# A hybrid decoder step on one core: the cached values multiplied unsplit in full precision, instead of as high and low parts

## The chip, the cores and the metric

The kernel runs on one core of a Trainium2 chip. TensorE (PE) multiplies, VectorE (DVE), ScalarE (ACT) and GpSimd (POOL) work element by element, SyncE (SP) issues most transfers. Each engine takes its own instructions in order, and the engines wait for one another through semaphores. The metric is the device time of one execution in microseconds (us); lower is better. The kernel before took 1194.81 us, the median of three runs (1193.85 to 1203.77).

## The reference

One layer of a decoder serves 512 prompt tokens and 8 sample sequences of one new token each. After a norm and one input projection, two mixers run side by side, and their results are gated, merged, projected and sent through an MLP. The part that matters here is the second mixer of the samples: softmax attention over 2048 cached positions (16 pages of 128), of which each head of each sequence sees the three best blocks of 256.

```
scores = einsum('bhqd,bhnd->bhqn', qh, k_mean);  top_k(scores, 3)
p = softmax(concat([q . k_selected, q . k_own]) * HD_B ** -0.5)
o = einsum('bhqkl,bhqkld->bhqd', p_sel, v_sel) + einsum('bhql,bhld->bhqd', p_own, v_own)
```

All is float32. There are 8 heads of 64, so a page of values is 128 positions x 512. The first mixer, a gated delta rule over the 512 prompt tokens in 4 chunks of 128 and 4 heads of 128, runs on the engines in the same stage.

## The kernel before, in words

The program has these stretches. The input units (29 of them, each a 1024 x 128 slice of weights times 520 columns) come first, to about 225 us. Prompt attention follows, with the products of cached keys and queries on POOL and their sums on DVE, to 344 us. Then come gates, the choice of blocks and the exponentials of the sample scores, to 394 us. Then the stage that the change touches, from 403 to 623 us: the four chunks of the delta rule, with the 64 value groups woven in. After it come the remaining gates with the sample recurrence, the merge, the output projection and the MLP.

Large products use a split: every weight tile `w_raw` is copied by ACT to `w_high` (type float32r, `split_high`, L400) and DVE writes the rest, `w_low` (`split_low`, L405). A product is then three float32r matmuls per slice (`product`, L416): high times high, high times low, low times high. Tiles of type float32, without such a split, are multiplied directly; the trace shows each of these matmuls as two records, while a float32r matmul is one.

The cached values go the same way. `ring` has four slots; each holds a group of two pages (2 x 128 x 512). SP loads a group (L509, L494) once its slot is free. For each group:

- ACT copies it to `v_high` (L827), which has two buffers,
- POOL (even groups, L574) or DVE (odd groups, L1261) writes `v_low`, the difference, and this frees the slot,
- PE multiplies both parts (L1782). The stationary operand is `wz`, 128 columns wide: the first 16 are the high and low parts of the 8 heads' unnormalised probabilities of that page, the rest are whatever follows them. The moving operand is 512 columns of `v_high` or `v_low`. That makes four matmuls a group.

After the 8 groups of a sequence, DVE keeps of the 16 x 512 sums the 64 columns of each row's own head (L1275), and PE adds the rows up by 4 small matmuls (`turn_values`, L1763).

The order is written out by hand. `delta_order` lists the stages of the delta rule for chunks 0 and 2 in one slot and 1 and 3 in the other, the second slot four steps behind. After the stages that `VALUES` names, each engine takes one value group; what is left of the 64 comes at the end of the stage. In the delta rule each `left` (4 matmuls, 128 columns each) needs DVE's last update of `Em` (L1333), and each `right` (8 matmuls) needs ACT's copy of `left` to `sqb` (L867); all of these are L1795 on PE.

The buffers `v_high` and `v_low` lie in the memory of `w_raw`. For this reason the weights of gates 8 to 11 are loaded from ACT's queue only after the last value matmul (`load_last_gates`), and gate 8 follows when they are split. `wz`, `sqb` and one of the buffers for the sums lie in the memory of `w_high` and `w_low`.

Of the kernel before, what the change touches and what calls it, by code (L numbers as in the profile page):

```python
# [26 lines left out]
ALU = mybir.AluOpType  # L27
# [135 lines left out]
def hybrid_step(nc, const_f, const_m, x_prompt, x_sample, cache_k, cache_v, page_table, state_delta, state_conv,  # L163
# [9 lines left out]
    with ExitStack() as ctx:  # L173
# [11 lines left out]
        v_high = at("v_high", [P, 2, 2 * WB], F32R, pos[0] - 16384)  # L185
        v_low = at("v_low", [P, 2, 2 * WB], F32R, pos[0] - 8192)
# [5 lines left out]
        wz = at("wz", [P, 2048 + 128], F32R, split_at + 4096)  # L192
# [125 lines left out]
        def bc(ap, shape):  # L318
# [21 lines left out]
            hw_out yf_sums yf_root yf_inv ys_out ys_done y_act y_dve v_scaled vb_masked vb_turned vb_out diag_out v_high_out v_low_pool v_low_dve""".split()  # L340
# [5 lines left out]
                lg_biased row_sums den_out gc_out ssr_in wz_low row_head sm_conv sm_ms sm_bd sm_decay sm_dlt sm_bdo  # L346
                sm_oms sm_on os_ready os_l inv_ready""".split(),
            "scalar": """sig_out sp_out tail_out lg_exp own_exp egc_out ssr_out wz_high wz_end sm_silu sm_root sm_bdin
# [15 lines left out]
        def done(name):  # L364

            engine, i = once_at[name]
            return once_sem[engine], i + 1
# [75 lines left out]
        def low_done(i):  # L443


            return S["v_low_dve" if i % 2 else "v_low_pool"], i // 2 + 1
# [7 lines left out]
        def _(sp):  # L454
# [47 lines left out]
            for r in range(8):  # L502
                if r < 4:
                    sp.wait_ge(S["k_red"], GROUPS - 3 + r)
                else:
                    sp.wait_ge(*low_done(r - 4))
# [45 lines left out]
        def _(g):  # L552
# [14 lines left out]
            values_done = [0]  # L567

            def values(n):

                for i in range(values_done[0], min(values_done[0] + n, GROUPS)):
                    if i % 2 == 0:
                        g.wait_ge(S["v_high_out"], i + 1)
                        g.tensor_tensor(v_low[:, i % 2], ring[:, i % 4].rearrange("p g c -> p (g c)"),  # L574
                                        v_high[:, i % 2].bitcast(F32), ALU.subtract).then_inc(S["v_low_pool"], 1)
                values_done[0] += n
# [18 lines left out]
            values(GROUPS)  # L595
# [9 lines left out]
        def _(act):  # L605
# [196 lines left out]
            for c in range(NCH):  # L802
# [9 lines left out]
            A(wz[:, 0:2048].rearrange("p (b g a h) -> p b g a h", b=NS, g=NPAGE, a=2)[:, :, :, 0],  # L812
              lg[:].rearrange("p b h g -> p b g h"), ACT.Copy).then_inc(*did("wz_high"))
            A(wz[:, 2048:], cf[:, K_ONE:K_ONE + P], ACT.Copy).then_inc(*did("wz_end"))

# [3 lines left out]
            values_done = [0]  # L819

            def values(n):

                for i in range(values_done[0], min(values_done[0] + n, GROUPS)):
                    act.wait_ge(kv_landed[i % 4], 32 * (2 * NS + i // 4 + 1))
                    if i >= 2:
                        act.wait_ge(S["pv_done"], i - 1)
                    A(v_high[:, i % 2], ring[:, i % 4].rearrange("p g c -> p (g c)"), ACT.Copy)\  # L827
                        .then_inc(S["v_high_out"], 1)
                values_done[0] += n
# [7 lines left out]
            values(1)  # L837
            taken, loaded = 0, False
            for stage, c in delta_order():
# [3 lines left out]
                values(VALUES.get(stage.rstrip("0123456789"), 0))  # L843
                if taken >= GROUPS and not loaded:
                    load_last_gates()
                    loaded = True
                taken += VALUES.get(stage.rstrip("0123456789"), 0)
# [39 lines left out]
            values(GROUPS)  # L887
            if not loaded:
                load_last_gates()


# [90 lines left out]
        def _(v):  # L982
# [259 lines left out]
            def head4(ap):  # L1242
                return ap.rearrange("p (h d) -> p h d", h=HA)

            v.wait_ge(*done("wz_high"))
            parts = wz[:, 0:2048].rearrange("p (b g a h) -> p b g a h", b=NS, g=NPAGE, a=2)
            TT(parts[:, :, :, 1], lg[:].rearrange("p b h g -> p b g h"), parts[:, :, :, 0].bitcast(F32), ALU.subtract)\
                .then_inc(*did("wz_low"))

            row_head = s5[0:2 * HB, 0:HB]  # L1250
            TT(row_head, cf[0:2 * HB, K_ID:K_ID + HB], cf[0:2 * HB, K_ID + HB:K_ID + 2 * HB], ALU.add)\
                .then_inc(*did("row_head"))
            v.wait_ge(*done("row_head"))
            values_done, lows_done = [0], [0]

            def lows(n):

                for i in range(lows_done[0], min(lows_done[0] + n, GROUPS)):
                    if i % 2:
                        v.wait_ge(S["v_high_out"], i + 1)  # L1260
                        TT(v_low[:, i % 2], ring[:, i % 4].rearrange("p g c -> p (g c)"),  # L1261
                           v_high[:, i % 2].bitcast(F32), ALU.subtract).then_inc(S["v_low_dve"], 1)
                lows_done[0] += n

            def values(n):

                for i in range(values_done[0], min(values_done[0] + n, GROUPS)):
                    b, r = divmod(i, 8)
                    lows(1)
                    if r == 7:  # L1270

                        v.wait_ge(S["pv_done"], i + 1)
                        if b >= 2:
                            v.wait_ge(S["vb_turned"], b - 1)
                        TT((vb0, vb1)[b % 2][0:2 * HB].rearrange("r (h d) -> r h d", d=DB),  # L1275
                           bank(2 + b % 2, WB, 2 * HB).rearrange("r (h d) -> r h d", d=DB),
                           bc(row_head.rearrange("r (h o) -> r h o", o=1), [2 * HB, HB, DB]), ALU.mult)\
# [9 lines left out]
            lows(1)  # L1287
# [245 lines left out]
        def _(pe):  # L1533
# [225 lines left out]
            def turn_values(b):  # L1759

                pe.wait_ge(S["vb_masked"], b + 1)
                for c in range(4):
                    last = mm(bank(2 + b % 2)[:, c:c + 1], (vb0, vb1)[b % 2][0:2 * HB, c * P:(c + 1) * P],  # L1763
                              cf[0:2 * HB, K_ONE:K_ONE + 1], start=True, stop=True, skip_group_check=True)
                last.then_inc(S["vb_turned"], 1)

            def values(n):
# [3 lines left out]
                for g in range(values_done[0], min(values_done[0] + n, GROUPS)):  # L1771
# [3 lines left out]
                    pe.wait_ge(*low_done(g))  # L1775
                    if g == 0:
                        pe.wait_ge(*done("wz_end"))
                        pe.wait_ge(*done("wz_low"))
                    for i in range(2):
                        first = (b * NPAGE + 2 * r + i) * 2 * HB  # L1780
                        for v_part in (v_high, v_low):
                            last = mm(bank(2 + b % 2), wz[:, first:first + P],  # L1782
                                      v_part[:, g % 2, i * WB:(i + 1) * WB],
                                      start=(r == 0 and i == 0 and v_part is v_high),
                                      stop=(r == 7 and i == 1 and v_part is v_low), skip_group_check=True)
# [230 lines left out]
```

## Time and profile before

| | |
|---|---|
| median of three runs | 1194.81 us |
| the profiled execution, its own time | 1196.35 us |
| span of its instructions | 1194.5 us |
| mean granted TensorE clock in it | 0.938 |
| PE busy | 1087.3 us (91%) |
| DVE, ACT, POOL busy | 648.0, 468.7, 256.4 us |
| the value matmuls L1782, 256 of them | 61.3 and 54.2 us busy |
| `v_high` copies L827, 64 | 67.2 us |
| `v_low` on POOL L574, 32 | 80.3 us |

Busy time of PE overlaps between neighbouring matmuls, because their ends are modelled; the distance from one start to the next tells what one costs in a stream. The granted clock is given as a share of 2.4 GHz, so 0.50 is 1.2 GHz. The profiled execution took 1.5 us more than the median.

### The profile page before, as it was taken

To read this page: it belongs to the slowest core of one execution; us is meant where nothing else is said; L and a number is where in the kernel's file an instruction comes from. 1 tells how busy PE (TensorE), PEld (TensorE's weight loads), DVE (VectorE), ACT (ScalarE), POOL (GpSimd) and SP (SyncE) were. 2 spreads that over 40 slices of the span, in tenths; PEclk is the share of its full clock that TensorE was granted. 3 is DMA by queue.
4 is the path that set the end of the run, shared out by engine and by line. 5 is a ranking of instruction groups with operands and counts; after the bars stand their busy time and mean duration, and the time that the engine had idled before them with its cause. 6 is when DMAs were issued, how large, how long until landed. Compare 5 with 4: busy or idle time off the path is not lost.

```text
span 1194.5 us, 21266 instructions
## 1 busy us (share of the span) xinstructions
PE 1087.3 (91%) x8054; PEld 1013.5 (85%) x8054; DVE 648.0 (54%) x892; ACT 468.7 (39%) x707; POOL 256.4 (21%) x113
## 2 busy tenths in 40 slices
PE   6999899698988589879968999999999999999997
PEld 6999799665677479668758799999999999999997
DVE  5228987897725774676544426555433433433443
ACT  6423554324333544554534122234413413523443
POOL 0035566776300353353330000000000000000000
PEclk8999899858998899989978899999999999999999
DMA  8376777655410245644547115433333332223311
GB/s 283 93 238 197 247 222 208 202 163 169 139 38 1 53 141 150 178 132 141 161 135 190 53 44 170 127 105 89 89 89 89 99 96 88 88 88 90 100 56 72
DMA packets 179256, 152.67 MB, mean 128 GB/s; under 512 B 8913, under 2 KB 141723, under 8 KB 178918
## 3 DMA queue, kind: packets, MB, share of 16 engines
q1 hardware_dynamic: 137414, 124.72, 35.5%
q10 hardware_dynamic: 41768, 26.91, 7.9%
q8 instruction: 52, 0.85, 0.3%
q14 instruction: 22, 0.18, 0.0%
HBM read 142.77 MB, written 8.93 MB: 127 GB/s over the span
## 4 chain that ended last, share of the span: by engine, by line
PE 76%; DVE 11%; ACT 5%; issue 4%; POOL 2%; ACTq 1%; DVEq 0%; POOLq 0%
PE ps L416 57%; PE ps L1795 6%; PE ps L1782 3%; DVE lg L1029 2%; POOL v_low L574 2%; PE ps L1682 1%; PE ps L1696 1%; DVE w_low L405 1%; PE ps L1539 1%; PE ps L1672 1%; ACTq L390 1%; DVE v_low L1261 1%; ACT v_high L827 1%; PE ps L1902 1%; ACT w_high L400 1%
## 5 line engine op out<-in xcount | busy, mean ns | idle before, releaser
L400 ACT ACTIVATE w_high<-w_raw 128x1024 fp32r<-128x1024 f32 x125 | 132.5, 1060 | 423.1 <-PE ps L416 399.8
L416 PE MATMUL ps<-xh,w_high 128*128 128x256 f32 x1216 | 257.5, 294 | 13.3 <-DVE w_low L405 7.4
L405 DVE TENSOR_TENSOR w_low<-w_raw,w_high 128x1024 fp32r<-128x1024 f32 x125 | 160.4, 1284 | 193.9 <-ACT w_high L400 193.6
L416 PE MATMUL ps<-xl,w_high 128*128 128x256 f32 x1216 | 250.0, 288 | 0.0
L416 PE MATMUL ps<-xh,w_low 128*128 128x256 f32 x1216 | 249.6, 287 | 0.0
L416 PEld LDWEIGHTS ps<-xh,w_high 128*128 128x128 f32 x1216 | 193.3, 194 | 21.1 <-issue 20.2
L416 PEld LDWEIGHTS ps<-xl,w_high 128*128 128x128 f32 x1216 | 193.7, 193 | 0.0
L416 PEld LDWEIGHTS ps<-xh,w_low 128*128 128x128 f32 x1216 | 193.6, 193 | 0.0
L557 POOL TENSOR_TENSOR ring<-ring,qb 128x1024 f32<-128x1024 f32 x64 | 158.5, 2488 | 158.7 <-DMA ring<-in_cache_k 87.0
L416 PE MATMUL ps<-mh,w_high 128*128 128x256 f32 (+1 forms) x640 | 129.3, 283 | 2.4 <-issue 2.4
L416 PE MATMUL ps<-mh,w_low 128*128 128x256 f32 (+1 forms) x640 | 129.5, 284 | 0.0
L416 PE MATMUL ps<-ml,w_high 128*128 128x256 f32 (+1 forms) x640 | 129.5, 284 | 0.0
L574 POOL TENSOR_TENSOR v_low<-ring,v_high 128x1024 fp32r<-128x1024 f32 x32 | 80.3, 2510 | 202.6 <-ACT v_high L827 202.6
L599 POOL TENSOR_TENSOR ys<-ys,rstd 8x1024 f32<-8x1024 f32 x1 | 1.9, 1886 | 566.8 <-DVE rstd L1523 566.8
L416 PEld LDWEIGHTS ps<-mh,w_high 128*128 128x128 f32 x640 | 99.8, 189 | 2.5 <-issue 2.5
L416 PEld LDWEIGHTS ps<-ml,w_high 128*128 128x128 f32 x640 | 99.9, 189 | 0.0
L416 PEld LDWEIGHTS ps<-mh,w_low 128*128 128x128 f32 x640 | 99.7, 189 | 0.0
L827 ACT ACTIVATE v_high<-ring 128x1024 fp32r<-128x1024 f32 x64 | 67.2, 1053 | 43.3 <-PE ps L1782 43.0
L1782 PE MATMUL ps<-v_high,wz 128*128 128x512 f32 x128 | 61.3, 479 | 18.1 <-DVE v_low L1261 9.0
L1029 DVE TENSOR_REDUCE lg<-ring 128x16 f32<-128x1024 f32 x64 | 76.2, 1211 | 0.1
L1502 DVE TENSOR_TENSOR ht<-ps,ht 128x520 f32<-128x520 f32 x32 | 22.4, 700 | 98.2 <-PE ps L416 98.2
L1782 PE MATMUL ps<-v_low,wz 128*128 128x512 f32 x128 | 54.2, 424 | 0.0
(358 smaller groups left out, 1498.0 us busy)
## 6 DMA issues: line engine op xcount, KB each, us to landing
ring<-in_cache_k SPq DMA_DIRECT2D x128, 256.0 KB, 3.0
ring<-in_cache_v SPq DMA_DIRECT2D x128, 256.0 KB, 2.9
w_raw<-in_w_in ACTq DMA_DIRECT2D x74, 256.0 KB, 4.0
w_raw<-in_w_up SPq DMA_DIRECT2D x64, 256.0 KB, 3.1
w_raw<-in_w_down SPq DMA_DIRECT2D x64, 256.0 KB, 2.9
w_raw<-in_w_in SPq DMA_DIRECT2D x16, 256.0 KB, 7.4
w_raw<-in_w_out SPq DMA_DIRECT2D x16, 256.0 KB, 3.0
ht_dram<-ht ACTq DMA_DIRECT2D x1, 2080.0 KB, 14.2
```

Source lines behind the costliest of these rows:

```text
L390: eng.dma_start(w_raw[:, u % 4, 4 * half:4 * half + 4, :], src).then_inc(w_landed[u % 4], 16)
L400: act.activation(w_high[:, u % 2], w_raw[:, s], ACT.Copy).then_inc(S_hi, 1)
L405: dve.tensor_tensor(w_low[:, u % 2], w_raw[:, u % 4], w_high[:, u % 2].bitcast(F32), ALU.subtract).then_inc(S_lo, 1)
L416: last = pe.matmul(out[:, a:b], w[:, u % 2, k, :], x[:, i, a:b], start=(first + i == 0 and w is w_high and x is rhs_h), stop=(first + i == ...
L557: g.tensor_tensor(ring[:, r % 4], ring[:, r % 4], bc(qb[:, b:b + 1, :], [P, 2, WB]), ALU.mult)\
L574: g.tensor_tensor(v_low[:, i % 2], ring[:, i % 4].rearrange("p g c -> p (g c)"), v_high[:, i % 2].bitcast(F32), ALU.subtract).then_inc(S[" ...
L827: A(v_high[:, i % 2], ring[:, i % 4].rearrange("p g c -> p (g c)"), ACT.Copy)\
L1029: v.tensor_reduce(lg[:, b, :, 2 * r:2 * r + 2].rearrange("p h g -> p g h"), ring[:, i % 4].rearrange("p g (h d) -> p g h d", d=DB), AX.X, ...
L1261: TT(v_low[:, i % 2], ring[:, i % 4].rearrange("p g c -> p (g c)"), v_high[:, i % 2].bitcast(F32), ALU.subtract).then_inc(S["v_low_dve"], 1)
L1502: TT(ht[:, j], unit_ps((U_MLP + i) % 2), ht[:, j], ALU.add).then_inc(S["h_out"], 1)
L1782: last = mm(bank(2 + b % 2), wz[:, first:first + P], v_part[:, g % 2, i * WB:(i + 1) * WB], start=(r == 0 and i == 0 and v_part is v_high) ...
L1795: last = mm(bank(out)[:, h * P:(h + 1) * P], left(h), right(h), start=(i == 0), stop=(i == len(pairs) - 1), skip_group_check=True)
```

## The change

The values are multiplied as they come. `v_high`, `v_low` and `wz` go, with ACT's 64 copies, the 32 subtractions on POOL and the 32 on DVE, the two copies and one subtraction that fill `wz`, and the small sum that makes `row_head`. PE waits for the landed transfer itself. The stationary operand is the 8 probabilities `lg[:, b, :, page]`, 8 columns with a step of 16 elements, the moving operand the 512 float32 columns of a page: two float32 matmuls a group instead of four float32r matmuls. Their sums have 8 rows, not 16. A slot of the ring is free when PE has multiplied it (`pv_done`). Since `w_raw` is free during the stage, ACT issues the weight loads of gates 8 to 11 before it.

```diff
-        v_high = at("v_high", [P, 2, 2 * WB], F32R, pos[0] - 16384)
-        v_low = at("v_low", [P, 2, 2 * WB], F32R, pos[0] - 8192)
-        wz = at("wz", [P, 2048 + 128], F32R, split_at + 4096)
-        def low_done(i):
-            return S["v_low_dve" if i % 2 else "v_low_pool"], i // 2 + 1
+        def slot_free(i):
+            return S["pv_done"], i + 1
...
                     if b is not None:
-                        taken, count = low_done(r + 4)
-                        sp.wait_ge(taken, b * 4 + (count - 4))
+                        sp.wait_ge(S["pv_done"], b * 8 + (r - 3))
...
-            values(1)
             for stage, c in delta_order():
-                values(VALUES.get(stage.rstrip("0123456789"), 0))
...
-            A(wz[:, 0:2048]...[:, :, :, 0], lg[:].rearrange("p b h g -> p b g h"), ACT.Copy)
-            A(wz[:, 2048:], cf[:, K_ONE:K_ONE + P], ACT.Copy).then_inc(*did("wz_end"))
-                    A(v_high[:, i % 2], ring[:, i % 4].rearrange("p g c -> p (g c)"), ACT.Copy)\
-                        .then_inc(S["v_high_out"], 1)
-            def load_last_gates():
-                act.wait_ge(S["pv_done"], GROUPS)
-                for u in range(U_GATE + 8, U_GATE + 12):
-                    load_unit(act, u)
+            for u in range(U_GATE + 8, U_GATE + 12):
+                load_unit(act, u)
             for stage, c in delta_order():
...
-            row_head = s5[0:2 * HB, 0:HB]
-            TT(row_head, cf[0:2 * HB, K_ID:K_ID + HB], cf[0:2 * HB, K_ID + HB:K_ID + 2 * HB], ALU.add)
+            row_head = cf[0:HB, K_ID:K_ID + HB]
-                        TT(v_low[:, i % 2], ring[:, i % 4].rearrange("p g c -> p (g c)"),
-                           v_high[:, i % 2].bitcast(F32), ALU.subtract).then_inc(S["v_low_dve"], 1)
...
-                    pe.wait_ge(*low_done(g))
-                    if g == 0:
-                        pe.wait_ge(*done("wz_end"))
-                        pe.wait_ge(*done("wz_low"))
+                    pe.wait_ge(kv_landed[g % 4], 32 * (2 * NS + g // 4 + 1))
                     for i in range(2):
-                        first = (b * NPAGE + 2 * r + i) * 2 * HB
-                        for v_part in (v_high, v_low):
-                            last = mm(bank(2 + b % 2), wz[:, first:first + P],
-                                      v_part[:, g % 2, i * WB:(i + 1) * WB], ...)
+                        last = mm(bank(2 + b % 2, WB, HB), lg[:, b, :, 2 * r + i], ring[:, g % 4, i, :],
+                                  start=(r == 0 and i == 0), stop=(r == 7 and i == 1), skip_group_check=True)
                     last.then_inc(S["pv_done"], 1)
```

On PE, the middle of the stage before, among the `left` and `right` steps of the delta rule (`Em,An` is a `left`, `sqb,Dm` and `Dm,sqb` a `right`):

```order
L1795 MATMUL ps<-sqb,Dm 128x128 x4
L1795 MATMUL ps<-Dm,sqb 128x128 x4
L1782 MATMUL ps<-v_high,wz 128x512
L1782 MATMUL ps<-v_low,wz 128x512
L1782 MATMUL ps<-v_high,wz 128x512
L1782 MATMUL ps<-v_low,wz 128x512
```

The same place now:

```order
L1718 MATMUL ps<-sqb,Dm 128x128 x4
L1718 MATMUL ps<-Dm,sqb 128x128 x4
L1707 MATMUL ps<-ring,lg 8x512 x2
L1718 MATMUL ps<-sqb,Dm 128x128 x4
L1718 MATMUL ps<-Dm,sqb 128x128 x4
L1707 MATMUL ps<-ring,lg 8x512 x2
```

The value group stays where it was; it is two instructions with 8 rows of sums where it was four. In both programs the 64 groups stand in 57 places, between other matmuls.

On ACT, the start of the stage before, from the last square root ahead of it:

```order
L809 ACTIVATE qks<-qks 128x32
L812 ACTIVATE wz<-lg 128x128x8
L814 ACTIVATE wz<-cf 128x128
L827 ACTIVATE v_high<-ring 128x1024 x3
L850 ACT_TABLE_LOAD
L850 ACTIVATE An<-An 128x512
```

And its end before:

```order
L827 ACTIVATE v_high<-ring 128x1024 x3
L390 DMA w_raw<-in_w_in 128x4x128 x8
L893 DMA state<-in_state_delta 128x32x128
L400 ACTIVATE w_high<-w_raw 128x1024 x2
L899 ACT_TABLE_LOAD
```

The start now:

```order
L790 ACT_TABLE_LOAD
L790 ACTIVATE qks<-qks 128x32
L387 DMA w_raw<-in_w_in 128x4x128 x8
```

The eight loads of gate weights have moved from behind the last value group to ahead of the first exponential of the stage, where the copies to `wz` and `v_high` stood.

## Rows read from the trace of the kernel before

**Rows 1.** Stretches: length, busy PE, PEld, DVE, ACT, POOL, clock, DMA share, GB/s.

```profile
394.40:403.40 9.00, 0.00 (x1) 0.00 (x0) 5.58 (x7) 6.02 (x7) 2.95 (x1) 0.75 0.00 0
403.40:622.60 219.20, 188.55 (x1184) 160.71 (x1184) 139.25 (x206) 107.26 (x140) 92.89 (x43) 0.93 0.51 144
```

**Rows 2.** The chain that ended last, in the stage: start, us, what.

```profile
461.00 0.93 PE ps L1782 x4
461.93 1.78 PE ps L1795 x16
```

**Rows 3.** Waits of PE from 403.4 to 623 us: total, times, longest.

```profile
PE ps L1813 <- DVE sqb L1296: 12.8, 4, 9.1
PE ps L1782 <- DVE v_low L1261: 9.0, 8, 2.2
PE ps L1782 <- POOL v_low L574: 8.7, 8, 2.7
PE ps L1539 <- DVE sqb L1358: 4.9, 4, 2.4
```

**Rows 4.** Stretches at half clock.

```profile
439.80:443.20 3.40, 3.40 (x18) 3.32 (x17) 0.00 (x0) 0.60 (x1) 1.26 (x1) 0.51 0.52 152
...
610.50:620.80 10.30, 8.00 (x22) 5.27 (x20) 3.81 (x8) 3.58 (x4) 2.50 (x2) 0.50 0.15 46
...
624.20:637.80 13.60, 6.21 (x29) 6.15 (x30) 4.54 (x9) 3.98 (x6) 0.00 (x0) 0.50 1.10 295
```

**Rows 5.** Timeline of POOL and DVE; then a DVE group: busy us, mean ns.

```profile
408.44 2.37 POOL L574 TENSOR_TENSOR v_low<-ring,v_high 128x1024 fp32r<-128x1024 f32 x1 [5.88 <-ACT v_high L827]
...
408.48 2.87 DVE L1312 TENSOR_TENSOR sqb<-tm,egc 128x512 f32<-128x512 f32 x1
...
L1358 DVE TENSOR_TENSOR sqb<-ps,on_st 128x512 f32<-128x512 f32 x4 | 2.8, 691 | 0.1
```

**Rows 6.** Timeline of PE around a `turn_values`: start, us, instruction.

```profile
448.52 0.40 PE L1782 MATMUL ps<-v_low,wz 128*128 128x512 f32 x1
448.85 1.05 PE L1763 MATMUL ps<-cf,vb 16*128 16x1 f32 x8
449.82 2.05 PE L1795 MATMUL ps<-Em,An 128*128 128x128 f32 x16
```

**Rows 7.** Timeline of PE in prompt attention, full clock.

```profile
326.78 1.09 PE L1696 MATMUL ps<-probt,mtv 128*64 128x128 f32 x8
327.80 1.16 PE L1682 MATMUL ps<-dg,prob 128*128 128x128 f32 x8
328.89 0.69 PE L1672 MATMUL ps<-kt,qt 64*128 64x512 f32 x1
```

**Rows 8.** Stretches, and the matmuls in them that fill few columns or few rows.

```profile
347.70:351.10 3.40, 3.40 (x18) 2.89 (x16) 0.00 (x0) 1.43 (x1) 0.00 (x0) 0.50 0.00 0
351.10:354.50 3.40, 3.40 (x31) 3.40 (x29) 0.00 (x0) 0.01 (x1) 0.00 (x0) 1.00 0.55 130
...
675.40:678.80 3.40, 3.40 (x5) 1.31 (x4) 1.75 (x3) 0.00 (x0) 0.00 (x0) 0.50 0.52 154
...
347.28 2.35 PE L1722 MATMUL ps<-cf,tail 128*11 128x128 f32 x12 [3.39 <-DVE onb_l L1124]
...
673.64 12.34 PE L1902 MATMUL ps<-bd,knt 32*128 32x512 f32 x16 [0.84 <-DVE bd L1409]
```

**Rows 9.** Timeline of DVE just ahead of the stage.

```profile
397.21 0.18 DVE L1233 TENSOR_TENSOR ckb<-nbeta,egc 128x16 f32<-128x16 f32 x1
```

**Rows 10.** Timeline at its end.

```profile
622.62 5.44 ACTq L390 DMA_DIRECT2D w_raw<-in_w_in  x8
...
629.33 2.00 ACT L400 ACTIVATE w_high<-w_raw 128x1024 fp32r<-128x1024 f32 x2 [1.08 <-issue]
...
631.90 0.78 PE L416 MATMUL ps<-xh,w_high 128*128 128x256 f32 x2 [7.39 <-DVE w_low L405]
```

**Rows 11.** The page, part 6: transfers, count, KB each, us to landing.

```profile
ring<-in_cache_v SPq DMA_DIRECT2D x128, 256.0 KB, 2.9
```

More of the change, by code:

```diff
@@ L339, in hybrid_step @@
             mh_out ml_out h_out sq2_out ssum_ready hx_h hx_l rel_out relsq_out uu_ready uh_out ul_out yt_turned
-            hw_out yf_sums yf_root yf_inv ys_out ys_done y_act y_dve v_scaled vb_masked vb_turned vb_out diag_out v_high_out v_low_pool v_low_dve""".split()
+            hw_out yf_sums yf_root yf_inv ys_out ys_done y_act y_dve v_scaled vb_masked vb_turned vb_out diag_out""".split()
         S = {n: sem(n) for n in names}
@@ L345, in hybrid_step @@
             "vector": """fw_out scr_out masks_out rope_q ba_out own_out sp_in gate_ready sel_red bias_ready
-                lg_biased row_sums den_out gc_out ssr_in wz_low row_head sm_conv sm_ms sm_bd sm_decay sm_dlt sm_bdo
+                lg_biased row_sums den_out gc_out ssr_in sm_conv sm_ms sm_bd sm_decay sm_dlt sm_bdo
                 sm_oms sm_on os_ready os_l inv_ready""".split(),
-            "scalar": """sig_out sp_out tail_out lg_exp own_exp egc_out ssr_out wz_high wz_end sm_silu sm_root sm_bdin
+            "scalar": """sig_out sp_out tail_out lg_exp own_exp egc_out ssr_out sm_silu sm_root sm_bdin
                 sm_t1o sm_osq sm_oroot sm_oh os_h""".split(),
@@ L505, in _ @@
                 else:
-                    sp.wait_ge(*low_done(r - 4))
+                    sp.wait_ge(*slot_free(r - 4))
                 for i in range(2):
@@ L565, in wide @@
                 return bc(ap.rearrange("p (h o) -> p h o", o=1), [P, HA, DA])
[L567 to L576, printed above, removed]
-            values(1)
             for stage, c in delta_order():
-                values(VALUES.get(stage.rstrip("0123456789"), 0))
                 if stage == "turn":
@@ L594, in _ @@
                     g.tensor_tensor(k, k, wide(ckb[:, c]), ALU.mult).then_inc(S["k_ready"], 1)
-            values(GROUPS)
             g.wait_ge(S["ys_out"], 1)
@@ L842, in _ @@
                 n_lv = (LEVELS - 1) * rep + lv
[L843 to L847, printed above, removed]
                 if stage == "decays":
@@ L886, in _ @@
                     A(ona_h[:, :, c * P:(c + 1) * P], An[:, p], ACT.Copy).then_inc(S["ona_h_out"], 1)
-            values(GROUPS)
-            if not loaded:
-                load_last_gates()
             act.wait_ge(S["ona_l_out"], NCH)
@@ L1243, in head4 @@
                 return ap.rearrange("p (h d) -> p h d", h=HA)
[L1245 to L1248, printed above, removed]
-            row_head = s5[0:2 * HB, 0:HB]
[L1251 to L1260, printed above, removed]
-                        TT(v_low[:, i % 2], ring[:, i % 4].rearrange("p g c -> p (g c)"),
-                           v_high[:, i % 2].bitcast(F32), ALU.subtract).then_inc(S["v_low_dve"], 1)
-                lows_done[0] += n
+            row_head = cf[0:HB, K_ID:K_ID + HB]
+            values_done = [0]
             def values(n):
@@ L1268, in values @@
                     b, r = divmod(i, 8)
-                    lows(1)
                     if r == 7:
@@ L1274, in values @@
                             v.wait_ge(S["vb_turned"], b - 1)
-                        TT((vb0, vb1)[b % 2][0:2 * HB].rearrange("r (h d) -> r h d", d=DB),
-                           bank(2 + b % 2, WB, 2 * HB).rearrange("r (h d) -> r h d", d=DB),
-                           bc(row_head.rearrange("r (h o) -> r h o", o=1), [2 * HB, HB, DB]), ALU.mult)\
+                        TT((vb0, vb1)[b % 2][0:HB].rearrange("r (h d) -> r h d", d=DB),
+                           bank(2 + b % 2, WB, HB).rearrange("r (h d) -> r h d", d=DB),
+                           bc(row_head.rearrange("r (h o) -> r h o", o=1), [HB, HB, DB]), ALU.mult)\
                             .then_inc(S["vb_masked"], 1)
@@ L1762, in turn_values @@
                 for c in range(4):
-                    last = mm(bank(2 + b % 2)[:, c:c + 1], (vb0, vb1)[b % 2][0:2 * HB, c * P:(c + 1) * P],
-                              cf[0:2 * HB, K_ONE:K_ONE + 1], start=True, stop=True, skip_group_check=True)
+                    last = mm(bank(2 + b % 2)[:, c:c + 1], (vb0, vb1)[b % 2][0:HB, c * P:(c + 1) * P],
+                              cf[0:HB, K_ONE:K_ONE + 1], start=True, stop=True, skip_group_check=True)
                 last.then_inc(S["vb_turned"], 1)
```

15 lines of the change are left out of this document (removed).

## The prediction

> **What bounds the kernel now.** I first cut the span into stretches. The change touches one of them and its two edges: PE stands still for 9.0 us before the stage [rows 1], the stage itself is 219.2 us, and 9.3 us pass from its last value matmul to gate 8 [rows 1, 10]. In those 219.2 us DVE, ACT and POOL are busy 139, 107 and 93 us, PE nearly 189. So PE sets the pace, with gaps.
>
> Second, the chain of waits through the stage. In its middle it runs on PE alone: a value group's four matmuls 0.93 us, then the 16 records of eight full float32 products of 128 columns 1.78 us [rows 2]. By these, the 392 products of the delta rule that stand in the program's order (L1795) are 87 us and the 64 value groups 59.5. The transposes, the four wide products of L1813 and the small ones of L1763 add some 20, by my estimate at the same rate per record. Together 167 of 219 us.
>
> Third, what the other 52 us are. PE waits 9.0 and 8.7 us for `v_low`, and 4.9 and 3.7 us (12.8 less the first, 9.1) for two results of DVE in the delta rule [rows 3]. Several stretches ran at half clock: four of 3.4 us like the first row, and the last 10.3 us [rows 4]. Work that PE does there costs double: 4 x 1.6, 4.0 from the 8.0 busy us of the last, and some 3 at the start, 13 us together. The last 12 or so are small waits and spaces between matmuls, which stay.
>
> **The change, part by part.**
>
> *The value matmuls.* A group now streams 2 x 512 float32 columns. Eight full products of 128 columns are as many columns, and take 1.78 us [rows 2]. That is the price from above; from below 1.70, since four records of 512 columns load fewer weights than sixteen of 128. I take 1.74, against 0.93 now: 64 x 0.81 = **+51.8 us** (49 to 54.4). PE is the pace, so it lies on the path.
>
> *Going to a narrow operand and back.* The new matmuls fill 8 of 128 columns. The trace has no stream of float32 matmuls like that, but has neighbours. Between value matmuls and the 16-row matmuls of `turn_values` the start comes 0.33 us after the last value matmul, against 0.23 within a group, and the eight small ones take 0.97 where 8 records take 0.89 [rows 6]. In prompt attention eight records on 64 columns take 1.02 us, and the eight full ones behind them 1.09, both 0.89 elsewhere [rows 7]: 0.13 and 0.20 for a change of shape. The groups stand in 57 places, each with a change in and out. The bounds are 0 (the change of shape hides) and 0.35 a place, both rows together; I take 0.2, as small weights also load sooner: 57 x 0.2 = **+11.4** (0 to 20).
>
> The Trainium skill (TensorEngine Tiling (Array Packing), Key Properties) says that a change of tiling mode drains the engine, which speaks against this change. By the drain that TensorE: Matmul & The Clock Gate (Step-by-step) gives, about 128 cycles, 114 changes would cost an estimated 6 us and the sum would be 5 less; the rows show more than that for a change, so I stay with them.
>
> *The waits for `v_low`* go: **-17.7** [rows 3]. They hide no other late thing for long, because each group is also 0.8 us longer and gives the delta rule that time.
>
> *The waits behind DVE*, 8.6 us. An operation on DVE that begins with a POOL subtraction takes 2.87 us, where the same shape takes 0.69 [rows 5], and POOL now has none of the 32 subtractions. DVE also loses 32 subtractions of 1.2 us out of the middle of its chains, ACT 64 copies. With the longer groups as cover I let **-8** go; at worst 4 come back.
>
> *Half clock.* The stretches at half clock in the middle follow upon gaps of PE, most of which close. I let 10 of the 13 us go: **-10** (-5 to -13). The 4 us left over in the last two terms are the start's.
>
> *The start.* DVE's last step that remains ends at 397.4, the stage starts at 403.4 [rows 9, 1]. In between stand DVE's part of `wz`, `row_head` and their waits. What is left is one product of 0.69, so PE starts at 398.1: **-5.3**. The eight weight loads now stand ahead of ACT's first exponential; their issue took 5.4 us [rows 10], and the `wz` and `v_high` copies that leave the place took 4.2, so ACT is free near 402. The exponential then needs a table load of 1.3 and the sums of DVE, ready near 401; PE meanwhile has the transposes and two groups. I cost this at nothing; without that cover it is 1 to 2 us.
>
> *The end.* The 9.3 us to gate 8 were issue and landing of its weights to 629.3, then split 2.6 [rows 10]. The weights are now there. The split still waits for the last sums to be turned, 1.9 us, and DVE first does four small products and a sum of the sample convolution. I take 5.6 in place of 9.3: **-3.7** (0 to -5). Gate 8 runs at half clock until 637.8 [rows 4], which costs 3 us; with the shorter gap half of that goes: **-1.5**.
>
> *The ring.* SP now waits for PE's product, not for DVE's or POOL's subtraction, so a slot comes free later by up to two groups. A transfer lands 2.9 us after its issue [rows 11], the second of a group 0.4 later, and three other groups lie between, at least 3 x 1.74 = 5.2 us. Cost nothing; the cover is thinnest in the last four groups, which stand alone.
>
> Sum: 51.8 + 11.4 - 17.7 - 8 - 10 - 5.3 - 3.7 - 1.5 = **+17.0**. I held the 12 us of small spaces fixed; with more work on PE they will close a little, and I take 2 us for that: **+15**. From the profiled execution (1196.35, 1.5 above the median) that makes 1211.4, from the median 1209.8. I say **1210**. The likeliest case's own range is 1203 to 1220.
>
> **The rivals.**
>
> *The groups cost only their columns, and the stage closes up.* A change to 8 columns costs nothing, as between neighbouring full shapes, and the delta rule's waits are covered. The mechanism is in the 57 places; below 0.05 us a place it decides. For it: small operands load faster. Against it: rows 6 and 7. The sum without the 11.4 is 3.6, and with another 1 to 3 us of spaces closed about +1 to +3: **1197**, not slower. Chance 0.24. To be faster by over 1% the stage would need to end some 14 us below that sum as well; nothing in the rows gives that. I leave 0.03.
>
> *Few columns count as few rows do for the clock.* The run of matmuls that fill 32 rows kept PE busy without a break, and yet the clock is at 0.50 in it [rows 8]. If 8 columns did the same, much of the stage would run at 1.2 GHz: 167 + 63 = 230 us of PE work twice, 1210 + some 200 = **1410**. Against it: twelve transposes that fill 11 columns and all rows take half of a stretch at 0.50, and the next stretch has 1.00 [rows 8]. Rows left empty lowered the clock, columns left empty did not stop its rise. Chance 0.06.
>
> The Trainium skill (TensorE: Matmul & The Clock Gate, What's actually happening) says that the clock follows how busy PE has been. By that the change could only help the clock; but PE was busy without a break on 32 rows and the clock fell, so I don't rest on it.
>
> *A new wait: the ring runs dry.* Slots come free only as PE ends a group, and 2 MB of gate weights are ahead of the ring's transfers at the start. The stage moves 144 GB/s on average [rows 1]; in runs of short stages PE would take groups faster. Each of some ten dense places would wait about 1.5 us: +15, **1225**. Against it: the landing of 2.9 us. Chance 0.07.
>
> *The change does less than it says*: the stage paces itself by DVE and the longer groups vanish into the gaps. PE's busy 189 of 219 us speak against it. It would give the first rival's time, and its chance is in there.
>
> **How the numbers follow.** Forecast 0.60, the closing rival 0.24, ring 0.07, clock 0.06, faster 0.03. The range leaves out the clock case and the faster one and the ends of the others: 1195 to 1229. A difference under 1%, about 12 us, can't be told from none. The forecast case lies above 1206.8 in some 0.85 of its chance, 0.51; with ring and clock, slower is 0.64. Same is 0.24 + 0.09 = 0.33, faster 0.03.
>
> **What would show it.** The stage's records of the value matmuls should start 0.43 us apart within a group; the distance from the last of a group to the start of the next product less 0.43 is the price of the change of shape. PE should wait for no ring transfer, and under 4 us for DVE. The clock should be 1.00 from the first group on. PE should start near 398, the stage end near 643 and gate 8 follow 5 to 6 us later. The prediction is wrong if a group costs far from 1.94 us, if the clock falls within the stage, or if PE's gaps stay.

## The result, and the profile after

| | before | changed |
|---|---|---|
| median, runs | 1194.8 us, 16 (1190.3 to 1203.8) | 1208.2 us, 16 (1201.2 to 1213.5) |
| ratio to before, 95% interval | | 1.0109 [1.0088, 1.0129] |
| profiled execution | 1196.35 us | 1213.45 us |
| its span, mean granted clock | 1194.5 us, 0.938 | 1211.6 us, 0.946 |
| PE busy | 1087.3 us (91%) | 1142.0 us (94%) |
| DVE, ACT, POOL busy | 648.0, 468.7, 256.4 us | 593.3, 403.0, 173.5 us |

The changed kernel is slower by 13.4 us, 1.1% (0.9 to 1.3, or 10.5 to 15.4 us). The forecast was 1210.

The profiled execution of the changed kernel is 17 us longer than that of before, and 6.9 us of this lies before the change: gate 7 ends at 401.3, not 394.4, since more of prompt attention ran at half clock in this one execution (57.8 us in one stretch, where the kernel before has 33.6 and then 3). The clock by fortieths of the span, of before and then of the changed kernel, differs ahead of the change in the eighth and the tenth place (the change begins in the fourteenth):

```profile
PEclk8999899858998899989978899999999999999999
```

```profile
PEclk8999899756998999999998989999999999999999
```

In the twelve kernels below, which share that code, gate 7 ends between 391.8 and 399.4, with no relation to the edit. So I read the stage by its own length, and the time by the medians.

The same view as [rows 1], the changed kernel, from the first product of the stage to the last `turn_values`; under it the kernel before, cut at the same two instructions. The columns are length, busy PE, PEld, DVE, ACT, POOL, clock, DMA share, GB/s:

```profile
405.16:644.28 239.12, 235.43 (x1184) 126.94 (x1184) 87.54 (x175) 45.89 (x79) 11.30 (x11) 0.99 0.50 142
```

```profile
403.45:623.36 219.91, 188.55 (x1184) 160.68 (x1184) 139.88 (x207) 107.26 (x140) 92.89 (x43) 0.93 0.51 144
```

The stage grew by 19.2 us, with PE busy nearly all of it and the clock at 0.99. It begins 3.9 us after gate 7, not 9.05, and gate 8 follows 4.9 us behind the start of the last `turn_values`, not 8.5. Together that is +10.3; the medians say +13.4. From the start of gate 8 on the two spans have 562.6 and 562.5 us.

PE's waits from 390 to 650 in the changed kernel, the answer to [rows 3] (total, times, longest):

```profile
PE ps L1736 <- DVE sqb L1226: 4.4, 2, 3.9
PE ps L413 <- DVE w_low L402: 3.8, 1, 3.8
PE ps L1469 <- DVE sqb L1288: 1.6, 1, 1.6
PE ps L1693 <- DVE vb L1206: 0.8, 1, 0.8
...
```

The first line, but for 0.5 us, and the second are the stage's edges; within it PE waits 3.7 us in all, and never for the ring. PE's timeline in the middle of the stage (start, busy us, instruction):

```profile
423.70 1.89 PE L1707 MATMUL ps<-ring,lg 128*8 128x512 f32 x4
425.52 1.16 PE L1718 MATMUL ps<-sqb,Dm 128*128 128x128 f32 x8
426.51 1.06 PE L1718 MATMUL ps<-Dm,sqb 128*128 128x128 f32 x8
427.50 1.89 PE L1707 MATMUL ps<-ring,lg 128*8 128x512 f32 x4
429.32 1.09 PE L1469 MATMUL ps<-cf,tm 128*128 128x128 f32 x8
430.25 0.60 PE L1469 MATMUL ps<-cf,sqb 128*128 128x128 f32 x4
430.69 1.06 PE L1718 MATMUL ps<-Em,An 128*128 128x128 f32 x8
431.58 0.61 PE L1718 MATMUL ps<-Em 128*128 128x128 f32 x4
```

Read the distances between starts. Eight full records are 0.89 apart where nothing narrow stands beside them (430.69 to 431.58), and 0.99 on either side of a group. A group takes 1.82 to the next start, where 1.72 is what wide_f32 below gives for full width. This is the change of shape: 0.1 us three times, ahead of the group, in it and behind it. (The last row ends with the window asked for; its product has eight records too.)

### The profile page after: what moved, and what is told of

It reads as the page before. It is cut to its first block, busy times and chain, and to the rows that moved or that the text cites. A ratio compares the mean times of both kernels' runs of the same rounds, so it can differ in the third digit from the quotient of the medians.

```text
span 1211.6 us, 21097 instructions
## 1 busy us (share of the span) xinstructions
PE 1142.0 (94%) x8054; PEld 984.1 (81%) x8054; DVE 593.3 (49%) x858; ACT 403.0 (33%) x641; POOL 173.5 (14%) x81
## 4 chain that ended last, share of the span: by engine, by line
PE 85%; DVE 8%; ACT 3%; issue 2%; ACTq 1%; DVEq 0%
PE ps L413 55%; PE ps L1707 9%; PE ps L1718 8%; PE ps L1602 2%; PE ps L1612 2%; DVE lg L978 2%; PE ps L1626 2%; PE ps L1469 2%; DVE w_low L402 2%; ACT w_high L397 1%; PE ps L1825 1%; ACTq L387 1%; PE ps L1508 1%; PE ps L1693 1%; DVE cvr L1008 1%
## 5 line engine op out<-in xcount | busy, mean ns | idle before, releaser
L402 DVE TENSOR_TENSOR w_low<-w_raw,w_high 128x1024 fp32r<-128x1024 f32 x125 | 163.8, 1311 | 188.4 <-ACT w_high L397 188.0
L1707 PE MATMUL ps<-ring,lg 128*8 128x512 f32 x256 | 121.0, 600 | 0.0
L978 DVE TENSOR_REDUCE lg<-ring 128x16 f32<-128x1024 f32 x64 | 76.2, 1210 | 0.1
L1707 PEld LDWEIGHTS ps<-ring,lg 128*8 128x8 f32 x256 | 19.3, 94 | 59.0 <-issue 53.0
L1263 DVE COPY_PREDICATED Em<-cm,ps 128x512 f32<-128x512 uint8 x24 | 17.5, 729 | 67.1 <-PE ps L1718 67.1
L1612 PE MATMUL ps<-dg,prob 128*128 128x128 f32 x160 | 32.6, 347 | 16.5 <-DVE dg L1082 16.4
```

What stands on the lines that cost most here:

```text
L402: dve.tensor_tensor(w_low[:, u % 2], w_raw[:, u % 4], w_high[:, u % 2].bitcast(F32), ALU.subtract).then_inc(S_lo, 1)
L978: v.tensor_reduce(lg[:, b, :, 2 * r:2 * r + 2].rearrange("p h g -> p g h"), ring[:, i % 4].rearrange("p g (h d) -> p g h d", d=DB), AX.X, ...
L1612: last = mm(bank(2 + n % 2)[:, t * P:(t + 1) * P], prob[:, n % 2, t * P:(t + 1) * P], dg[:, n % 2], start=True, stop=True, skip_group_chec ...
L1707: last = mm(bank(2 + b % 2, WB, HB), lg[:, b, :, 2 * r + i], ring[:, g % 4, i, :], start=(r == 0 and i == 0), stop=(r == 7 and i == 1), sk ...
```

## The experiments

Each was compared with the kernel before on the same chip; the medians of before in these comparisons are 1193.4 to 1198.4 us. They stand by question, not in the order in which they ran.

### Is it the shape? wide_f32

The edit: ACT copies the probabilities to a contiguous `wz` of float32, once, ahead of the stage, and the matmuls take 128 columns of it; nobody reads the sums of the last 120.

```diff
-  mm(bank(2 + b % 2, WB, HB), lg[:, b, :, 2 * r + i], ring[:, g % 4, i, :], ...)
+  mm(bank(2 + b % 2), wz[:, first:first + P], ring[:, g % 4, i, :], ...)
```

> The changed kernel, with the 8 probabilities copied to a buffer where 128 columns can be read from them, so that the float32 value matmuls fill all columns. Theory (the change of shape costs 0.29 us in each of the 57 places, as the trace of the changed kernel shows: entry 0.10, exit 0.20): 57 x 0.29 = 16.5 us less than 1208.2, and 128-column weights cost at most 0.02 a matmul more, 2.5: about 1194. Rival (the distances are a cost of going to and from long matmuls, not of the narrow shape): no change, 1208.

Measured: 1193.4 us (10 runs), ratio 0.9969 [0.9938, 1.0001]. With sixteen times the columns to load it is 15 us faster than the changed kernel. Its timeline:

```profile
442.81 1.88 PE L1714 MATMUL ps<-ring,wz 128*128 128x512 f32 x4
444.62 1.05 PE L1697 MATMUL ps<-cf,vb 8*128 8x1 f32 x8
...
448.44 1.06 PE L1725 MATMUL ps<-Dm,sqb 128*128 128x128 f32 x8
449.33 1.88 PE L1714 MATMUL ps<-ring,wz 128*128 128x512 f32 x4
451.05 1.05 PE L1725 MATMUL ps<-sqb,Dm 128*128 128x128 f32 x8
```

The eight records ahead of a group are back at 0.89, and the group is 1.72. Its stage:

```profile
401.43:627.32 225.89, 221.79 (x1184) 152.59 (x1185) 87.60 (x175) 46.26 (x81) 11.31 (x11) 0.99 0.53 150
```

It is 13.2 us shorter than the changed kernel's 239.12, by the width (or the layout) of the stationary operand alone. Over the 57 places that is 0.23 each on average.

Three times 0.1 in every place would be 17. The two stages have the same matmuls in the same order, so their starts can be compared one by one. Ahead of a group the changed kernel loses 0.1 us almost everywhere, 5.6 in all. In the group and behind it, it loses 0.19 in the 38 places where a product of the delta rule follows, but only 0.08 in the 11 where a transpose follows, and nothing in the 8 where `turn_values` follows. The stationary operand of `turn_values` is 8 columns wide in both kernels, and wide_f32 pays there too: 1.81 from 442.81 to 444.62. That makes 13.7; half a microsecond comes back in the long runs of value matmuls.

### Or the stride? packed_narrow, cols64_f32

wide_f32 had also removed the step of 16 elements between the probabilities. So one kernel takes 8 neighbouring columns of `wz`, another 64:

```diff
-  mm(bank(2 + b % 2), wz[:, first:first + P], ring[:, g % 4, i, :], ...)
+  mm(bank(2 + b % 2, WB, HB), wz[:, first:first + HB], ring[:, g % 4, i, :], ...)    # packed_narrow
+  mm(bank(2 + b % 2, WB, 64), wz[:, first:first + 64], ring[:, g % 4, i, :], ...)    # cols64_f32
```

> The changed kernel, but its 8 probabilities of a page are copied by ACT into 8 neighbouring columns ahead of the stage (in the changed kernel they stand 16 elements apart). In wide_f32 two things were altered at once: the width (128 columns for 8) and this stride. Theory (the shape): the price of a change of shape stays, 57 x 0.29 us, so the time stays near 1208 (1205 to 1211) and the eight records ahead of a group take 0.99 us. Rival (the stride): strided float32 weights are what loads slowly; then this kernel gives what wide_f32 gave, 1193 (1190 to 1197).

Measured: 1208.1 us (6 runs), ratio 1.0086 [1.006, 1.0112].

> wide_f32 with 64 columns in place of 128 (the last 56 are numbers that nobody reads). Theory: any operand that fills less than all 128 columns pays the change of shape, as the 64-column matmuls of prompt attention seemed to (0.13 and 0.20 us): 1205 to 1209. Rival: the price belongs to few columns only, and at 64 it is gone: 1192 to 1196. Between: 1197 to 1204, if it grows with the columns left empty.

Measured: 1208.0 us (6 runs), ratio 1.0081 [1.0052, 1.011]. A timeline of each:

```profile
420.80 1.88 PE L1714 MATMUL ps<-ring,wz 128*8 128x512 f32 x4
422.61 1.09 PE L1473 MATMUL ps<-cf,tm 128*128 128x128 f32 x8
...
428.56 1.16 PE L1725 MATMUL ps<-sqb,Dm 128*128 128x128 f32 x8
429.56 1.06 PE L1725 MATMUL ps<-Dm,sqb 128*128 128x128 f32 x8
430.55 1.88 PE L1714 MATMUL ps<-ring,wz 128*8 128x512 f32 x4
```

```profile
421.20 1.93 PE L1714 MATMUL ps<-ring,wz 128*64 128x512 f32 x4
423.06 1.16 PE L1725 MATMUL ps<-sqb,Dm 128*128 128x128 f32 x8
424.05 1.06 PE L1725 MATMUL ps<-Dm,sqb 128*128 128x128 f32 x8
```

Both have the 0.99 and the 1.8 again (with 64 columns 1.86). By the cut of the 239.12 their stages are 238.9 and 241.3 us. The stride is out, and the price is no smaller where fewer columns are left empty: 8 and 64 columns pay it, 128 do not.

The Trainium skill (TensorEngine Tiling (Array Packing), Key Properties) says that a change of tiling mode drains TensorE. A price per change between a part of the columns and all of them agrees with that; the page gives no figure for it. No run here shows that a drain is what happens in those 0.1 us, and the float32r matmuls of the next section, on 16 columns, pay nothing, which the sentence by itself does not foresee.

### And with float32r? before_narrow

The kernel before, with 16 columns of `wz` in place of 128.

```diff
-  last = mm(bank(2 + b % 2), wz[:, first:first + P], ...)
+  last = mm(bank(2 + b % 2, WB, 2 * HB), wz[:, first:first + 2 * HB], ...)
```

> The kernel before, its float32r value matmuls on the 16 columns that carry probabilities, instead of 128. Shape theory: 57 x 0.29 = 16.5 us more than 1194.8, less what its waits hide, 1203 to 1211, and no new stretch at half clock. Clock rival (empty columns let the clock fall): stretches at 0.50 in the stage and over 1230. Rival that narrowness is free: 1195.

Measured: 1191.7 us (10 runs), ratio 0.9971 [0.9926, 1.0016]. The shape theory's 1203 to 1211 missed; the rival that narrowness is free said 1195. The timeline, with 16 columns, and then the same place in the kernel before, with 128:

```profile
445.42 1.06 PE L1795 MATMUL ps<-Dm,sqb 128*128 128x128 f32 x8
446.23 0.48 PE L1782 MATMUL ps<-v_high,wz 128*16 128x512 f32 x1
...
447.24 1.05 PE L1795 MATMUL ps<-sqb,Dm 128*128 128x128 f32 x8
```

```profile
444.20 1.06 PE L1795 MATMUL ps<-Dm,sqb 128*128 128x128 f32 x8
445.01 0.48 PE L1782 MATMUL ps<-v_high,wz 128*128 128x512 f32 x1
...
446.03 1.05 PE L1795 MATMUL ps<-sqb,Dm 128*128 128x128 f32 x8
```

From the eight records ahead to the next product it is 0.81 + 1.01 = 1.82 with 16 columns and 0.81 + 1.02 = 1.83 with 128. So the price isn't one of narrow operands as such: float32 matmuls pay it, float32r ones here did not. The stage is 220.5 us, not 219.9, and its clock 0.93 in both, so the clock did not fall by the 16 columns either.

### The other way round: swapped

The 128 values of a slice are the stationary operand, the probabilities of two heads the moving one: 16 records a group of 2 columns each; the masking and turning of sums go.

```diff
-  mm(bank(2 + b % 2, WB, HB), lg[:, b, :, 2 * r + i], ring[:, g % 4, i, :], ...)
+  for c in range(4):
+      mm(bank(2 + b % 2)[:, 2 * c:2 * c + 2], ring[:, g % 4, i, c * P:(c + 1) * P],
+         lg[:, b, 2 * c:2 * c + 2, 2 * r + i], ...)
```

> The changed kernel, with the operands of the value matmuls changed over: the values are the stationary operand, 128 columns at a time, and 2 columns of probabilities move; the 64-column sums come out turned, so turn_values and the masking go. Theory: no narrow shape in the stage; a group is 16 records at 0.112 us, 1.79, against 1.72; saved 57 x 0.29 = 16.5 and 8 x 1.1 for turn_values, lost 64 x 0.07 = 4.5: about 20 us less, 1188. Rival (weights of 128 x 128 that change with each small matmul cost more than their 0.112, since nothing long covers them): 1208 or more.

Measured: 1247.2 us (4 runs), ratio 1.0396 [1.0314, 1.0478]. Missed by 59 us. Two stretches (columns as above):

```profile
400.00:640.00 240.00, 238.55 (x1701) 234.69 (x1702) 77.69 (x159) 43.60 (x72) 11.30 (x11) 0.80 0.44 125
...
427.00:433.00 6.00, 6.00 (x30) 6.00 (x30) 1.46 (x2) 0.00 (x0) 0.00 (x0) 0.50 0.26 90
```

PE has matmuls under way without a break, and weight loads beside them, and yet the granted clock is 0.80 over the stage. A group in a stretch at half clock and one at full, in the timeline:

```profile
430.43 3.41 PE L1702 MATMUL ps<-lg,ring 128*128 128x2 f32 x16
...
451.21 1.85 PE L1702 MATMUL ps<-lg,ring 128*128 128x2 f32 x16
```

At 1.00 the sixteen matmuls take 1.71 us to the next start, where the expectation said 1.79; the clock undid it. So the clock can fall with PE never idle, as the clock rival of the prediction held, but here it was with the other operand small: matmuls of 2 moving columns, each behind a full weight load. Which of the two lowered it, this run does not separate. Few stationary columns with 512 moving ones did not: the stage's clock is 0.99 with 8 and with 64, and with 16 it is 0.93, as with 128 in the same kernel.

The Trainium skill (TensorE: Matmul & The Clock Gate, What's actually happening) lets the clock follow how busy PE has been. In this stage PE shows no idle time and the clock fell; the measurement decides.

### What the low parts cost before: before_high_twice

The kernel before without the 64 subtractions; PE multiplies `v_high` twice, so its work is the same, and a slot of the ring is free after ACT's copy. It leaves out the low parts of the values and counts the high parts twice.

```diff
-  for v_part in (v_high, v_low):
+  for v_part, part_no in ((v_high, 0), (v_high, 1)):
...
-  g.tensor_tensor(v_low[:, i % 2], ...)     # POOL
-  TT(v_low[:, i % 2], ...)                  # DVE
```

> The kernel before without the low parts of the values: POOL and DVE don't subtract, PE multiplies the high part twice, so its work stays the same; the slot is free after ACT's copy. It shows what the waits for the low part, their restarts, the collisions of DVE with POOL and the half clock behind them cost together. Theory: 17.7 us of waits, 5 to 8 of waits behind DVE, 6 to 9 of half clock and some 8 of restarts that the page counts as busy: 35 to 40 less, about 1158. Rival (each is covered by something else that is late): 17.7 less or under, 1177 to 1190.

Measured: 1167.0 us (4 runs), ratio 0.9751 [0.9691, 0.981], 30 us less. PE's waits in the stage:

```profile
PE ps L1806 <- DVE sqb L1289: 8.3, 2, 6.9
PE ps L1532 <- DVE sqb L1351: 7.6, 4, 3.5
PE ps L416 <- DVE w_low L405: 7.2, 1, 7.2
PE ps L1775 <- ACT v_high L823: 2.3, 3, 1.8
```

The subtractions, with the waits that hang on them, cost the kernel before 30 us. The waits for `v_low`, in [rows 3] 17.7 us, are little more than half of it. The rest is half clock, spaces and the start: the stage's clock rose from 0.93 to 0.99, and the stage begins 2.1 us earlier. PE's other waits in the stage did not fall by 5 to 8 us, as the theory had it, but rose from 13.2 to 17.1, since the delta rule's own chain shows through when PE gets to it sooner (L1532, 7.6 us against 4.9). Together these account for the 9 us by which the theory's 1158 was too low.

### What a group is worth: half_values, double_values

The changed kernel with one page of each group not multiplied, and with each value matmul done twice; the first leaves out half of the values, the second counts them twice.

```diff
-  for i in range(2):        # half_values
+  for i in range(1):
...
+  for again in range(2):    # double_values
       last = mm(bank(2 + b % 2, WB, HB), lg[:, b, :, 2 * r + i], ring[:, g % 4, i, :], ...)
```

> The changed kernel with one page of each group left out of the value matmuls (both are loaded). Theory: 64 matmuls at 0.858 less, 55 us, if PE stays the pace; but the waits of the delta rule behind DVE and ACT that the long groups cover come back in part, some 5 to 10: 1158 to 1163. Rival (a group needs its length as cover): under half of 55 is gained, over 1180.

Measured: 1159.8 us (4 runs), ratio 0.9736 [0.9695, 0.9777].

> The changed kernel with each value matmul twice. Theory: all of the 128 added float32 matmuls lie on the path at 0.858 us: 110 us more, 1318. Rival (PE has gaps left that they fill): 1300 or less.

Measured: 1312.0 us (4 runs), ratio 1.0994 [1.0956, 1.1031]. Up, 110 us of added matmuls gave 104 by the medians and 106 by the ratios: PE is the bound. Down, 55 us less gave 48 or 45, since waits return, among them, for the first time, the ring's:

```profile
PE ps L1469 <- DVE sqb L1288: 4.8, 4, 1.6
...
PE ps L1707 <- DMA ring<-in_cache_v: 2.3, 3, 1.4
```

### The gate weights, POOL: late_gates, pool_busy

late_gates is the changed kernel with the eight loads of gates 8 to 11 back behind the last value matmul; pool_busy gives POOL 32 subtractions again, into a buffer nobody reads.

```diff
+  act.wait_ge(S["pv_done"], GROUPS)                               # late_gates, ahead of the four load_unit
+  g.wait_ge(S["pv_done"], i - 1)                                  # pool_busy, every even group
+  g.tensor_tensor(idle[:], flat, flat, ALU.subtract)
```

> The changed kernel, with the weight loads of gates 8 to 11 back behind the last value matmul. Theory: the 5.7 us from the last value matmul to gate 8 become 9.3 again, and ACT is free 5 us earlier at the start, which nobody waits for: 1208.2 + 3.6 = 1212. Rival: the early loads delay the first groups at the start by as much as they save at the end: 1208.

Measured: 1210.7 us (4 runs), ratio 1.0165 [1.0122, 1.0207]. PE waits 7.4 us before gate 8, not 3.8: the 3.6 us are there in the trace. The medians differ by 2.4 and the ratios by 6.7, less than these runs can tell apart.

> The changed kernel with 32 subtractions of 128x1024 back on POOL, at the places of before, to a buffer that nobody reads. It tells whether DVE's collisions with POOL cost time by themselves. Theory: DVE's operations that begin with one take up to 2.9 us again, but PE's longer groups cover most: 0 to 3 us more, 1208 to 1211, and waits of PE for DVE go from 2 us in the stage to 3 to 6. Rival (the collisions were the cause of the waits behind DVE in full): 8 more, 1216.

Measured: 1207.2 us (4 runs), ratio 1.0126 [1.0093, 1.016]. DVE is held up again: a small step just ahead of the stage takes 1.58 us, and 0.17 in the changed kernel, and of two like products one takes 2.38 us and one 0.68:

```profile
394.83 1.58 DVE L1200 TENSOR_SCALAR qks<-qks 128x16 f32<-128x16 f32 x1
...
410.01 2.38 DVE L1248 TENSOR_TENSOR tm<-tm,qks 128x512 f32<-128x512 f32 x1
412.32 0.68 DVE L1249 TENSOR_TENSOR tm<-tm,qks 128x512 f32<-128x512 f32 x1
```

PE pays for the first, as it stands idle there: its wait ahead of the stage is 5.3 us, not 3.9. In the stage nobody pays: it is 239.3 us by the same cut as the 239.12 above. Where PE is the bound, POOL's interference is covered. The Trainium skill (SBUF — State Buffer, SBUF: two separate sides) says that a VectorE instruction with two SBUF inputs and a GpSimd one that reads SBUF lock each other out for a whole instruction; 0.68 against 2.38 here, and 0.69 against 2.87 in [rows 5], agree.

### A kernel that beats both: every_other, one_in_four

If splitting costs waits and not splitting costs PE time, a mixture should cost less of both. The kernel before, with the even groups unsplit and 128 columns wide: the same `wz` read as float32, its 16 rows of sums the same. POOL does nothing there.

```diff
+  if g % 2 == 0:
+      last = mm(bank(2 + b % 2), wz[:, first:first + P].bitcast(F32), ring[:, g % 4, i, :], ...)
+      continue
   for v_part in (v_high, v_low):
       last = mm(bank(2 + b % 2), wz[:, first:first + P], v_part[:, g // 2 % 2, i * WB:(i + 1) * WB], ...)
```

> The kernel before with the even value groups multiplied unsplit (float32, all 128 columns of wz, straight from the ring); the odd groups are split by ACT and DVE as before, and POOL does no values. Theory (what hurt the kernel before was the pace of the splitting and POOL and DVE in each other's way, not PE's work): PE gets 32 x 0.81 = 26 us more; the waits for POOL (8.7) and most of those for DVE (9.0, 8) go, with some 10 us of half clock and half of the small spaces: 1180 (1174 to 1187), below both kernels. Rival (unsplit groups only ever trade a wait for work, as in wide_f32): 1191 to 1197.

Measured: 1186.6 us (6 runs), ratio 0.9913 [0.989, 0.9937], 10.7 us below before and some 22 below the changed kernel (by the medians 21.6, by the ratios 23). Its stage, and PE's waits:

```profile
400.40:612.50 212.10, 199.24 (x1184) 152.43 (x1184) 123.94 (x207) 74.70 (x108) 12.19 (x11) 0.99 0.53 149
```

```profile
PE ps L1819 <- DVE sqb L1295: 8.8, 2, 6.9
PE ps L416 <- DVE w_low L405: 7.2, 1, 7.2
PE ps L1538 <- DVE sqb L1357: 5.1, 4, 2.2
PE ps L1788 <- DVE v_low L1260: 3.7, 5, 2.2
```

The stage is 7.8 us shorter than before's 219.91 though PE has 32 x 0.79 = 25 us more to do in it, so 33 us of waits, late steps and half clock went. Against wide_f32's 225.89 it is 13.8 us shorter with 25 us less work: there splitting half of the groups costs 11.5 us of waits. The edit also gives each of the 32 split groups its turn in two buffers, so a part is needed again only four groups later, not two; what that is worth by itself is not shown. The start, against before, is 2.1 us shorter: a 16 x 8 sum of DVE takes 0.14 us where POOL's first subtraction had stretched it to 2.27.

> As every_other, but only every fourth group is unsplit; the odd groups are split by ACT and DVE, the others by ACT and POOL, with two buffers of each part in turn. Against every_other PE has 16 x 0.81 = 13 us less. If the waits and spaces of the kernel before grow evenly with the share of groups that is split (38 us from none to all, by wide_f32 against before), half of what every_other removed, some 10, comes back: 1183, a little below every_other. Rival (what hurts is POOL and DVE at the same time, and a buffer that each split group needs): nearly all of it comes back, and the time is 1188 to 1196, above every_other.

Measured: 1196.1 us (12 runs; before 1198.4 in this comparison), ratio 0.9983 [0.9954, 1.0012]: the rival's case. From half of the groups unsplit to a quarter, 13 us of PE work go and yet the time rises by 8 to 9 us, so some 21 us of waits, spaces and half clock came back. Its waits show about half of that, the two for `v_low` 13.3 us against 3.7:

```profile
PE ps L1804 <- DVE v_low L1276: 6.8, 7, 2.2
PE ps L1554 <- DVE sqb L1373: 6.7, 4, 2.5
PE ps L1804 <- POOL v_low L587: 6.5, 5, 1.6
```

and its clock from 405 to 600 is 0.96, against 1.00 in every_other:

```profile
405.00:600.00 195.00, 175.16 (x1109) 144.95 (x1108) 117.99 (x183) 81.25 (x112) 48.78 (x24) 0.96 0.53 149
```

Whether POOL or the two shared buffers did it, these two kernels don't separate.

## Why the prediction was right, point by point

The time (1210, measured 1208.2) and the case (slower, by PE's work and a change of shape that the waits which go don't pay back) were right. Of its terms:

- **Value matmuls, +51.8.** 1.72 us a group by the wide timeline, 1.74 forecast: 64 x 0.79 = 50.6. Right; double_values gives 104 of 110.
- **Change of shape, +11.4.** 13.2 us by the two stages, 0.23 a place, 0.2 forecast, with bounds of 0 and 0.35 (its two rows of prompt attention add up to 0.33). The reason for taking less than the rows (small weights load sooner) is not borne out: the loads are shorter, on average 94 ns with 8 columns, 137 with 64 and 193 with 128, but 64 columns cost as much as 8, and 128 nothing. So the size was right and its reason was not.
- **Waits for `v_low` and behind DVE, -25.7.** The 17.7 went. Of the 8.6 behind DVE 2.1 are left (L1469 and 0.5 of L1736), where the forecast left 0.6; with the smaller waits PE waits 3.7 us in the stage, under the 4 that were forecast.
- **Half clock, -10.** The stage's clock rose from 0.93 to 0.99. One stretch at 0.50 is left in it, 3.4 us at its start (405.7 to 409.1), which costs 1.7 of the 13, so about 11 went. Right.
- **The start, -5.3; the end, -3.7.** Measured -5.2 and -3.7 (8.5 to 4.9 from the last `turn_values`). Right.
- **Gate 8's half clock, -1.5.** It did not come. Gate 8 begins with 5.9 us at 0.50 in the kernel before and with 5.65 us in the changed one, and from its start the spans have 562.6 and 562.5 us. The shorter gap gave nothing back.
- **The small spaces, -2.** This is the term that was mis-sized. By the cut at 219.91 us the old stage had 166.5 us of work (59.5 + 107), 17.7 + 8.6 of waits and 13 for half clock, which leaves 14 of small waits and spaces, where the prediction held 12. The new one has 64 x 1.72 + 13.2 + 107 = 230.3 of work, 2.1 of those waits and 1.7 for half clock, which leaves 5. So some 9 closed, not 2. The stage ended at +19.2 where the terms gave +25.5 (51.8 + 11.4 - 17.7 - 8 - 10 - 2), and this term, 7 us short, makes the difference; the errors of the others nearly cancel. The 107 are the prediction's estimate. That the spaces were restarts behind the waits, and went with them, fits before_high_twice, where 30 us went with 17.7 of listed waits, but no run shows it by itself.

By the trace the change is +10.3 and by the medians +13.4 (10.5 to 15.4); the forecast of +15 lies above both, inside the interval. One trace of each kernel does not show where the 3 us between them lie. So it is in part luck that the forecast came within 2 us: the terms are 4.7 too high against the trace. And where the prediction said that a difference under 1% can't be told from none, 16 runs of each told this 1.1% from none to within 0.2.

The rivals: the closing one needed a change of shape that costs nothing; wide_f32 is its world, and gave 1193.4 where it said 1197. The ring did not run dry; it first shows with half of the value matmuls gone. The clock did not fall by few stationary columns.

## What to carry to other kernels

A run of float32 matmuls that fill only part of the columns, put between full ones, cost about a quarter of a microsecond a visit here; widening the stationary operand with numbers nobody reads removed it. And when a helper engine's work causes waits, taking half of that work back into the busy engine can beat both pure forms: here splitting the first half of the groups cost 11.5 us of waits, spaces and half clock in the stage and splitting the second half 33, and each saved PE 25.

## What the runs showed of the hardware

- float32: 8, 64 and 128 stationary columns gave 1208.1, 1208.0 and 1193.4 us. float32r: 16 and 128 gave 1191.7 and, in the same comparison, 1197.0 (ratio 0.9971 [0.9926, 1.0016]), no difference that can be told.
- Matmuls of 2 moving columns behind full weight loads, among full products, PE without a break: granted clock 0.80 over 240 us, 0.50 in a stretch of 6 us.
- Weight loads of 8, 64 and 128 float32 columns took 94, 137 and 193 ns on average, and yet the 128 were the cheapest to go to and come back from.
- The waits for `v_low` in the view are less than the subtractions cost: 17.7 us listed, 30 measured.
